# The last round of a triangular inverse in a two-layer kernel, computed on one 32x32 block a head instead of on masked 64x64 blocks

## The chip, the cores and the metric

The kernel runs on one core of a Trainium2 chip. The metric is device time in microseconds (us); three runs of the kernel before gave 3733.14, 3735.51 and 3737.32 us. The engines are called PE (tensor engine; its weight loads are PEld), DVE (vector engine), ACT (scalar engine), POOL (GpSimd) and SP (which issues the DMAs).

## The reference, cut to what matters

The program is two transformer-like blocks over 512 tokens of width 1024. The second block's even layer holds a recurrence with 12 heads of width 64, in two directions, over 768 tokens (256 of context and 512 of latents):

```
def rwkv7_scan(r, w, k, v, kk, bb, s0, reverse):
    def step(s, inp):
        r_t, w_t, k_t, v_t, kk_t, b_t = inp
        sa = jnp.einsum('bhij,bhj->bhi', s, kk_t)
        s = s * w_t[:, :, None, :] - sa[..., None] * b_t[:, :, None, :] + v_t[..., None] * k_t[:, :, None, :]
        return s, jnp.einsum('bhij,bhj->bhi', s, r_t)
```

The kernel does not step token by token. It cuts the tokens into 12 chunks of 64. Inside a chunk the term with `sa` couples each token to all tokens before it, which is a triangular system of 64 equations for each head; the kernel inverts its matrix (ones on the diagonal, a strictly triangular 64x64 part that holds products of `bb` and `kk`).

## The kernel before, in words

**Passes.** The function `rwkv` runs 12 passes, `products(i)`, one for each pair of heads `p` and direction `d` (`p, d = divmod(i, 2)`). The two heads of a pair lie in partitions 0 to 63 and 64 to 127, and `halves_matmul` issues one 64x64 product for each. Each pass is one `stage`: a block of all engines, closed by a barrier. The next pass begins on every engine only when the last engine has ended its part.

**Inside a pass.** First come the `units`, products whose results are masked and stored (`mats`, `ntrk`, `ax`, and `wb`). Then come 15 `rounds` of the inverse: 5 levels (block sizes 2, 4, 8, 16, 32) for each of 3 groups of 4 chunks. `buf.wb` holds for each chunk the inverse so far, transposed in columns 0 to 63 ("wt") and straight in columns 64 to 127. Round n of level b does this:

1. POOL: `off_diagonal(n)` multiplies the strict triangle in `mats` by a mask of the two off-diagonal bxb blocks of each 2bx2b block, into `off`.
2. PE: the Y product, `off` (weights) by the straight half of `wb`, into bank 0 or 1 of PSUM. The trace shows it as `second_wb,second_off`.
3. ACT: copies it to `y`.
4. PE, one turn of the loop later: the W product, `y` by `wt` (`second_wb,second_y`), and except in the last level also its straight twin (`second_y,second_wb`).
5. DVE: adds the result to `wb`. In the last level it adds only to the 64 columns of `wt`.

In the text Y(n), W(n) and mask(n) are these steps of round n; rounds 12, 13 and 14 are the last level. On PE the loop's order is Y(n), then what stands "beside", then W(n-1).

**Beside the rounds.** Two other pieces of work are dealt into fixed places of the same loop, on each engine: `Terms` (the elementwise terms of pass i+1, in long DVE instructions of 128x768) and `Recurrence` (the chunk-to-chunk state of pass i-1). A `step` of the recurrence is 12 small products on PE, then a `tensor_scalar` on DVE that makes the state `st` for the next step. Passes 1 to 10 have both; pass 0 has only `Terms`, pass 11 only `Recurrence`. The order in each engine's queue is fixed by this loop: no scheduler moves anything.

Of the kernel before, what the change touches and what calls it, by code (L numbers as in the profile page):

```python
# [11 lines left out]
ALU = mybir.AluOpType  # L12
# [26 lines left out]
N_SHIFT = 3 * RWKV_W + 256  # L39
CH = 64  # L40
NCH = T2 // CH
RET_HEADS = 8
DECAY = math.exp(-0.5)

# [14 lines left out]
def const_table():  # L59
# [46 lines left out]
    t["upper"] = np.concatenate([s < q, s <= q], 1)  # L106
    t["lower"] = np.concatenate([s > q, s >= q], 1)
    t["eye64"] = s == q
    for b in (1, 2, 4, 8, 16, 32):
        off = (s // (2 * b) == q // (2 * b)) * (s // b != q // b)  # L110
        t[f"up{b}"] = off * (s < q)
        t[f"lo{b}"] = off * (s > q)
# [1778 lines left out]
class Recurrence:  # L1891
# [33 lines left out]
    def slots(self, g):  # L1925
        first = slot_of(self.i, self.starts[g])
        return slice(first, first + 4)
# [134 lines left out]
def rwkv(nc, w, u_dram, o_dram, xc, common, psum, col, at, columns):  # L2062
# [4 lines left out]
    with ExitStack() as ctx:  # L2067
# [210 lines left out]
        def products(i):  # L2278
# [3 lines left out]
            ar, bk, starts = buf.ar[:, i % 3, :, :], buf.bk[:, i % 2, :, :], group_starts(d)  # L2282
            pair_mask = "upper" if d == 0 else "lower"
            pre_t, pre_f = ("up", "lo") if d == 0 else ("lo", "up")
            over = lambda name: mask(name).unsqueeze(1).to_broadcast([P, 4, mask(name).shape[1]])
            bank = lambda b, n: psum[:, b * 512:b * 512 + 4 * n].rearrange("p (c n) -> p c n", n=n)

# [11 lines left out]
            after_unit = lambda n: range(UNIT_PLACES * n // len(units), UNIT_PLACES * (n + 1) // len(units))  # L2299
            BANKS = 4  # L2300
            bank_y, bank_w = lambda n: bank(n % 2, CH), lambda n: bank(2 + n % 2, 2 * CH)
            names = "unit_ready taken_act taken_dve wt_scaled wt_begun wf_begun masked y_ready y_taken w_ready w_added "
            with stage(nc, names + Terms.NAMES + Recurrence.NAMES) as (block, sems):
                (unit_ready, taken_act, taken_dve, wt_scaled, wt_begun, wf_begun, masked, y_ready, y_taken, w_ready,
                 w_added) = sems[:11]
                terms = Terms(sems[11:11 + Terms.COUNT], i + 1, p - 1 if d == 1 and p else None)
                rec = Recurrence(nc, sems[11 + Terms.COUNT:], i - 1, buf, psum, eye)

                @block.sync
                def _(sp):  # L2310
# [3 lines left out]
                def _(pe):  # L2314
# [30 lines left out]
                    for n in range(len(rounds) + 1):  # L2345
                        if n < len(rounds):
                            level, g = rounds[n]
                            pe.wait_ge(masked, n + 1)
                            if level == 0:
                                pe.wait_ge(wf_begun, g + 1)  # L2350
                                pe.wait_ge(wt_begun, g + 1)
                            else:
                                pe.wait_ge(w_added, n - 2)
                            if n >= 2:
                                pe.wait_ge(y_taken, n - 1)
                            for c in range(4):
                                last = halves_matmul(nc, bank_y(n)[:, c, :], off[:, n % 2, c, :], buf.wb[:, slots(g).start + c, CH:])
                            last.then_inc(y_ready, 1)
                        beside(UNIT_PLACES + n)
                        if n:  # L2360
                            level, g = rounds[n - 1]
                            s0 = slots(g).start
                            pe.wait_ge(y_taken, n)
                            if n > 2:
                                pe.wait_ge(w_added, n - 2)
                            for c in range(4):
                                wt, y_ = buf.wb[:, s0 + c, 0:CH], y[:, own(g).start + c, :]
                                last = halves_matmul(nc, bank_w(n)[:, c, 0:CH], y_, wt)
                                if level < last_level:
                                    last = halves_matmul(nc, bank_w(n)[:, c, CH:], wt, y_)  # L2370
                            last.then_inc(w_ready, 1)

                @block.scalar
                def _(act):
# [18 lines left out]
                    for n in range(len(rounds) + 1):  # L2393
                        if n < len(rounds):
                            level, g = rounds[n]
                            act.wait_ge(y_ready, n + 1)
                            S.activation(y[:, own(g), :], bank_y(n), ACT.Identity).then_inc(y_taken, 1)  # L2397
                        beside(UNIT_PLACES + n)

                @block.vector  # L2400
                def _(dve):
# [19 lines left out]
                    for n in range(len(rounds) + 1):  # L2421
                        beside(UNIT_PLACES + n)
                        if n:
                            level, g = rounds[n - 1]
                            dve.wait_ge(w_ready, n)
                            n_cols = 2 * CH if level < last_level else CH
                            w_ = buf.wb[:, slots(g), 0:n_cols]
                            V.tensor_tensor(w_, w_, bank_w(n)[:, :, 0:n_cols], ALU.add).then_inc(w_added, 1)  # L2428

                @block.gpsimd  # L2430
                def _(pool):
# [18 lines left out]
                        for phase in terms.due(place, PLACES):  # L2450
                            terms.pool(pool, phase)
                    for n in range(len(rounds) + 1):
                        if 2 <= n < len(rounds):
                            off_diagonal(n)
                        for phase in terms.due(UNIT_PLACES + n, PLACES):
                            terms.pool(pool, phase)
# [512 lines left out]
```

## Time and profile before

| what | us |
|---|---|
| median of three runs | 3735.51 |
| the profiled execution, its time | 3739.27 |
| the profiled execution, its span from first to last instruction | 3737.5 |
| the stretch with the twelve passes (2360 to 3030 us of the span) | 670 |

A long name such as `L1881 PE MATMUL psum<-second_wb,second_off 64*64 64x64 f32` reads: line 1881, engine, operation, output, then the moving operand and the weights, the shape of the weights, and the shape of the moving operand. One product in f32 appears as two matmul records and two weight loads, so the 8 products of a group show as x16. Matmul records overlap their neighbours: a record's end is modelled, and the pace is read from the starts. `[0.78 <-DVE second_st L2022]` behind a row says that the engine had been idle for 0.78 us and that this DVE instruction released it.

### The profile page before, as it was taken

How to read it: one execution, taken by the hardware profiler on the slowest of the kernel's cores; microseconds unless marked ns; L12 is line 12 of the kernel's file. 1: busy time of each engine (PE TensorE's matmuls, PEld its weight loads, DVE VectorE, ACT ScalarE, POOL GpSimd, SP SyncE). 2: the span in 40 equal slices, each digit the busy share in tenths (PEclk: the TensorE clock that was granted, in tenths of full speed). 3: DMA queues.
4: the chain of work that ended last, by engine and by line, in shares of the span. 5: the costliest groups of instructions: out<-in, count | busy, mean ns of one | idle time of the engine just before them, and what ended most of it. 6: DMA issues, size and time to landing. Idle time of an engine off the chain costs nothing. (4 is left out here: it accounts for less than half of the span.)

```text
span 3737.5 us, 66286 instructions
## 1 busy us (share of the span) xinstructions
PE 3191.7 (85%) x28285; PEld 2513.8 (67%) x28285; DVE 1989.7 (53%) x2750; ACT 1124.0 (30%) x1783; POOL 1043.7 (28%) x608
## 2 busy tenths in 40 slices
PE   4998899999699988999855996799999978399886
PEld 2875567878476556887624884688888866279634
DVE  3678747860477874883204740566666632431252
ACT  2224424331323343332213221333333212322221
POOL 0322134544122222554200220444344311022100
PEclk7999899999899999999967998899999998799988
DMA  2331122333222122333171332000000021021101
GB/s 69 79 79 46 45 69 85 97 93 88 65 64 78 40 63 67 92 98 90 54 274 52 112 98 109 16 4 20 20 20 20 8 77 45 17 79 57 51 0 68
DMA packets 354104, 243.93 MB, mean 65 GB/s; under 512 B 22212, under 2 KB 330872, under 8 KB 353164
## 3 DMA queue, kind: packets, MB, share of 16 engines
q1 hardware_dynamic: 350398, 231.57, 20.7%
q10 hardware_dynamic: 3406, 8.04, 0.6%
q8 instruction: 227, 3.72, 0.4%
q14 instruction: 73, 0.60, 0.1%
HBM read 222.54 MB, written 17.04 MB: 64 GB/s over the span
## 5 line engine op out<-in xcount | busy, mean ns | idle before, releaser
L571 POOL TENSOR_TENSOR weights_lo<-weights_raw,weights_hi 128x1024 fp32r<-128x1024 f32 (+1 forms) x234 | 595.7, 2546 | 1151.4 <-ACT weights_hi L540 1151.4
L1167 PE MATMUL psum<-moving_hi,weights_hi 128*128 128x512 f32 x1488 | 609.0, 409 | 108.4 <-DVE weights_lo L571 61.3
L1167 PE MATMUL psum<-moving_lo,weights_hi 128*128 128x512 f32 x1488 | 589.0, 396 | 0.0
L1167 PE MATMUL psum<-moving_hi,weights_lo 128*128 128x512 f32 x1488 | 588.3, 395 | 0.0
L1167 PEld LDWEIGHTS psum<-moving_hi,weights_hi 128*128 128x128 f32 x1488 | 285.2, 192 | 226.2 <-issue 71.2
L540 ACT ACTIVATE weights_hi<-weights_raw 128x1024 fp32r<-128x1024 f32 (+2 forms) x250 | 253.7, 1019 | 280.5 <-PE psum L1167 240.4
L1167 PEld LDWEIGHTS psum<-moving_hi,weights_lo 128*128 128x128 f32 x1488 | 285.0, 192 | 61.8
L1167 PEld LDWEIGHTS psum<-moving_lo,weights_hi 128*128 128x128 f32 x1488 | 285.9, 192 | 59.2 <-issue 4.9
L2436 POOL TENSOR_TENSOR second_off<-second_mats,second_masks 128x256 f32<-128x256 f32 x180 | 141.1, 786 | 183.8 <-PE psum L1881 183.8
L1167 PE MATMUL psum<-hn_hi,even_hi 128*128 128x256 f32 (+1 forms) x480 | 162.9, 339 | 34.1 <-DVE even_lo L571 34.1
L571 POOL TENSOR_TENSOR even_lo<-even_raw,even_hi 128x1024 fp32r<-128x1024 f32 x28 | 67.4, 2408 | 362.8 <-ACT even_hi L540 362.8
L1881 PE MATMUL psum<-second_wb,second_y 64*64 64x64 f32 x2880 | 165.8, 218 | 0.4 <-issue 0.3
L1167 PE MATMUL psum<-hn_lo,even_hi 128*128 128x256 f32 (+1 forms) x480 | 162.7, 339 | 0.0
L1167 PE MATMUL psum<-hn_hi,even_lo 128*128 128x256 f32 (+1 forms) x480 | 162.4, 338 | 0.0
L2428 DVE TENSOR_TENSOR second_wb<-second_wb,psum 128x512 f32<-128x512 f32 (+1 forms) x180 | 113.2, 630 | 82.3 <-PE psum L1881 82.0
L719 DVE SCALAR_TENSOR_TENSOR cv<-u,columns,cv 128x512 f32<-128x512 f32 x88 | 154.8, 1759 | 3.1
L2397 ACT ACTIVATE second_y<-psum 128x256 f32<-128x256 f32 x180 | 68.7, 382 | 275.0 <-PE psum L1881 274.9
L1167 PE MATMUL psum<-hidden_hi,weights_hi 128*128 128x512 f32 x352 | 139.6, 397 | 7.5 <-POOL weights_lo L571 7.5
L1881 PE MATMUL psum<-second_y,second_wb 64*64 64x64 f32 x2304 | 141.9, 218 | 0.0
L1881 PEld LDWEIGHTS psum<-second_wb,second_y 64*64 64x64 f32 x2880 | 138.2, 135 | 1.7 <-issue 1.4
L1167 PE MATMUL psum<-hidden_lo,weights_hi 128*128 128x512 f32 x352 | 138.9, 395 | 0.0
L1167 PE MATMUL psum<-hidden_hi,weights_lo 128*128 128x512 f32 x352 | 138.9, 395 | 0.0
(430 smaller groups left out, 6890.1 us busy)
## 6 DMA issues: line engine op xcount, KB each, us to landing
weights_raw<-in_w_up SPq DMA_DIRECT2D x88, 512.0 KB, 3.9
weights_raw<-in_w_in SPq DMA_DIRECT2D x78, 512.0 KB, 3.8
ada_raw<-in_ada_w SPq DMA_DIRECT2D x12, 2048.0 KB, 18.6
odd_raw<-in_od_w_in SPq DMA_DIRECT2D x16, 1024.0 KB, 5.5
even_raw<-in_ev_w_in SPq DMA_DIRECT2D x30, 512.0 KB, 3.9
weights_raw<-in_w_down SPq DMA_DIRECT2D x32, 448.0 KB, 3.7
weights_raw<-in_w_o SPq DMA_DIRECT2D x16, 512.0 KB, 4.3
weights_raw<-in_w_down SPq DMA_DIRECT2D x16, 512.0 KB, 4.2
```

Of the source, the lines that this page charges most:

```text
L540: self.nc.scalar.activation(self.ring.hi[i % n][:, a:b], self.ring.raw[:, t % self.ring.landing, a:b], ACT.Identity)\
L571: ops.tensor_tensor(self.ring.lo[i % n][:, a:b], self.ring.raw[:, t % self.ring.landing, a:b], self.ring.hi[i % n][:, a:b].bitcast(F32), A ...
L719: nc.vector.scalar_tensor_tensor(y, x[:, 0:L], col("ffn_w", chunk), y, ALU.mult, ALU.add).then_inc(convolved, 1)
L1167: return nc.tensor.matmul(to, (hi, lo)[which][:, at:at + P], moving(k)[part], start=start and k == 0 and i == 0, stop=stop and k == n_k - ...
L1881: last = nc.tensor.matmul(out[ps, :], lhsT[ps, :], rhs[ps, :], start=start, stop=stop)
L2397: S.activation(y[:, own(g), :], bank_y(n), ACT.Identity).then_inc(y_taken, 1)
L2428: V.tensor_tensor(w_, w_, bank_w(n)[:, :, 0:n_cols], ALU.add).then_inc(w_added, 1)
L2436: G.tensor_tensor(off[:, n % 2, :, :], buf.mats[:, slots(g), 0:CH], over(f"{pre_t}{LEVELS[level]}"), ALU.mult)\
```

## The change

In the last level only one 32x32 block of the 64x64 matrix is off the diagonal and inside the triangle. The changed kernel computes only this block for each head. The Y product takes 32 rows and 32 columns of `mats` itself as weights, with no mask, and writes from one half of the head's partitions to the other half; the W product goes back the other way. ACT copies half as many columns. DVE copies the block into `wb`, where only zeros stand, in two instructions (one for each head, 32 partitions each) in place of one addition over 128 partitions. POOL's masks for rounds 12 to 14 and the two 64-column mask tables of block size 32 are gone. One more semaphore, `last_copied`, counts the copies.

```
+            first, other = (0, 1) if d == 0 else (1, 0)
+            half = lambda hf, j: slice(64 * hf + HB * j, 64 * hf + HB * j + HB)
+            columns_of = lambda j: slice(HB * j, HB * j + HB)
...
                         if n < len(rounds):
                             level, g = rounds[n]
-                            pe.wait_ge(masked, n + 1)
+                            if level < last_level:
+                                pe.wait_ge(masked, n + 1)
...
                             for c in range(4):
-                                last = halves_matmul(nc, bank_y(n)[:, c, :], off[:, n % 2, c, :], buf.wb[:, slots(g).start + c, CH:])
+                                x = slots(g).start + c
+                                if level < last_level:
+                                    last = halves_matmul(nc, bank_y(n)[:, c, :], off[:, n % 2, c, :], buf.wb[:, x, CH:])
+                                else:
+                                    for hf in range(2):
+                                        last = PE.matmul(bank_y(n)[half(hf, other), c, 0:HB], buf.mats[half(hf, first), x, columns_of(other)],
+                                                         buf.wb[half(hf, first), x, CH:][:, columns_of(first)], start=True, stop=True)
                             last.then_inc(y_ready, 1)
...
+                            adds = GROUPS * last_level
                             if n > 2:
-                                pe.wait_ge(w_added, n - 2)
+                                pe.wait_ge(w_added, min(n - 2, adds))
+                            if n - 2 > adds:
+                                pe.wait_ge(last_copied, 2 * (n - 2 - adds))
                             for c in range(4):
                                 wt, y_ = buf.wb[:, s0 + c, 0:CH], y[:, own(g).start + c, :]
-                                last = halves_matmul(nc, bank_w(n)[:, c, 0:CH], y_, wt)
                                 if level < last_level:
+                                    halves_matmul(nc, bank_w(n)[:, c, 0:CH], y_, wt)
                                     last = halves_matmul(nc, bank_w(n)[:, c, CH:], wt, y_)
+                                else:
+                                    for hf in range(2):
+                                        last = PE.matmul(bank_w(n)[half(hf, first), c, 0:HB], y_[half(hf, other), 0:HB],
+                                                         wt[half(hf, other), columns_of(other)], start=True, stop=True)
                             last.then_inc(w_ready, 1)
...
                             act.wait_ge(y_ready, n + 1)
-                            S.activation(y[:, own(g), :], bank_y(n), ACT.Identity).then_inc(y_taken, 1)
+                            n_cols = CH if level < last_level else HB
+                            S.activation(y[:, own(g), 0:n_cols], bank_y(n)[:, :, 0:n_cols], ACT.Identity).then_inc(y_taken, 1)
...
-                            n_cols = 2 * CH if level < last_level else CH
-                            w_ = buf.wb[:, slots(g), 0:n_cols]
-                            V.tensor_tensor(w_, w_, bank_w(n)[:, :, 0:n_cols], ALU.add).then_inc(w_added, 1)
+                            if level < last_level:
+                                w_ = buf.wb[:, slots(g), :]
+                                V.tensor_tensor(w_, w_, bank_w(n), ALU.add).then_inc(w_added, 1)
+                            else:
+                                for hf in range(2):
+                                    V.tensor_copy(buf.wb[half(hf, first), slots(g), columns_of(other)], bank_w(n)[half(hf, first), :, 0:HB])\
+                                        .then_inc(last_copied, 1)
...
                     for n in range(len(rounds) + 1):
-                        if 2 <= n < len(rounds):
+                        if 2 <= n < GROUPS * last_level:
                             off_diagonal(n)
```

On PE, near the end of pass 1: W(12), Y(14), step 10 of the recurrence, W(13). Before:

```order
L1881 MATMUL psum<-second_wb,second_y 64x64 x8
L1881 MATMUL psum<-second_wb,second_off 64x64 x8
L1881 MATMUL psum<-second_v_tok,second_mats 64x64 x2
L1881 MATMUL psum<-second_wau,second_mats 64x64 x2
L1881 MATMUL psum<-second_st,second_mr 64x64 x2
L1881 MATMUL psum<-second_ntrk,second_v_tok 64x64 x2
L1881 MATMUL psum<-second_mats,second_wau 64x64 x2
L1881 MATMUL psum<-second_mr,second_st 64x64 x2
L1881 MATMUL psum<-second_wb,second_y 64x64 x8
L1881 MATMUL psum<-second_v_tok,second_mats 64x64 x2
```

After (the line numbers move with the added lines):

```order
L2387 MATMUL psum<-second_wb,second_y 32x32 x8
L2367 MATMUL psum<-second_wb,second_mats 32x32 x8
L1882 MATMUL psum<-second_v_tok,second_mats 64x64 x2
L1882 MATMUL psum<-second_wau,second_mats 64x64 x2
L1882 MATMUL psum<-second_st,second_mr 64x64 x2
L1882 MATMUL psum<-second_ntrk,second_v_tok 64x64 x2
L1882 MATMUL psum<-second_mats,second_wau 64x64 x2
L1882 MATMUL psum<-second_mr,second_st 64x64 x2
L2387 MATMUL psum<-second_wb,second_y 32x32 x8
L1882 MATMUL psum<-second_v_tok,second_mats 64x64 x2
```

The places are the same; the three groups of 8 products of the last level are now 32x32, and they stand between groups of 64x64 products.

On DVE, in the same pass, the end of its queue: state 9, the result of W(12), a term of pass 2, state 10, W(13), a term, state 11, the output, W(14). Before:

```order
L2022 TENSOR_SCALAR second_st<-psum,second_decay 128x64
L2428 TENSOR_TENSOR second_wb<-second_wb,psum 128x4x64
L2237 TENSOR_TENSOR second_a<-second_kk,second_a 128x768
L2022 TENSOR_SCALAR second_st<-psum,second_decay 128x64
L2428 TENSOR_TENSOR second_wb<-second_wb,psum 128x4x64
L2239 TENSOR_TENSOR second_bk<-second_a,second_e 128x12x64
L2022 TENSOR_SCALAR second_st<-psum,second_decay 128x64
L2027 TENSOR_TENSOR second_o<-second_o,psum 128x256
L2428 TENSOR_TENSOR second_wb<-second_wb,psum 128x4x64
```

After:

```order
L2023 TENSOR_SCALAR second_st<-psum,second_decay 128x64
L2450 COPY second_wb<-psum 32x4x32 x2
L2238 TENSOR_TENSOR second_a<-second_kk,second_a 128x768
L2023 TENSOR_SCALAR second_st<-psum,second_decay 128x64
L2450 COPY second_wb<-psum 32x4x32 x2
L2240 TENSOR_TENSOR second_bk<-second_a,second_e 128x12x64
L2023 TENSOR_SCALAR second_st<-psum,second_decay 128x64
L2028 TENSOR_TENSOR second_o<-second_o,psum 128x256
L2450 COPY second_wb<-psum 32x4x32 x2
```

Each addition of 128x4x64 has become two copies of 32x4x32, in the same place of the queue.

## Rows read from the trace of the kernel before

**Rows 1.** Busy us (count) of PE, PEld, DVE, ACT, POOL; then PEclk, DMA share, GB/s
```profile
2360.00:3030.00 670.00, 621.94 (x16708) 577.23 (x16710) 417.94 (x666) 229.84 (x443) 275.98 (x310) 0.99 0.05 15
```

**Rows 2.** Groups of instructions in the same stretch; columns as on the page
```profile
L1881 PE MATMUL psum<-second_wb,second_off 64*64 64x64 f32 x2880 | 115.5, 218 | 3.4 <-POOL second_off L2436 2.1 <-issue 0.6 <-ACT second_ax L2390 0.6
...
L2436 POOL TENSOR_TENSOR second_off<-second_mats,second_masks 128x256 f32<-128x256 f32 x180 | 141.1, 786 | 183.8 <-PE psum L1881 183.8
...
L2428 DVE TENSOR_TENSOR second_wb<-second_wb,psum 128x256 f32<-128x256 f32 x36 | 15.0, 418 | 8.2 <-PE psum L1881 7.9
```

**Rows 3.** Timeline, tensor engine, end of a pass in direction 0; start us, us taken
```profile
2516.22 0.63 PE L1881 MATMUL psum<-second_wb,second_off 64*64 64x64 f32 x16
...
2521.27 0.63 PE L1881 MATMUL psum<-second_wb,second_y 64*64 64x64 f32 x15
...
2521.97 0.33 PE L1881 MATMUL psum<-second_v_tok,second_mats 64*64 64x64 f32 x4
...
2522.72 0.65 PE L1881 MATMUL psum<-second_wb,second_y 64*64 64x64 f32 x16
...
2524.40 1.15 PE L1881 MATMUL psum<-second_masks,second_bk 64*64 64x64 f32 x32 [1.04 <-PEq L187]
```

**Rows 4.** Timeline, vector engine and GpSimd, end of the same pass
```profile
2517.05 1.45 DVE L2235 SCALAR_TENSOR_TENSOR second_ar<-second_kk,second_e 128x768 f32<-128x768 f32 x1
...
2518.61 0.67 DVE L2428 TENSOR_TENSOR second_wb<-second_wb,psum 128x512 f32<-128x512 f32 x1
...
2520.30 0.42 DVE L2428 TENSOR_TENSOR second_wb<-second_wb,psum 128x256 f32<-128x256 f32 x1 [0.53 <-PE psum L1881]
...
2520.64 0.95 DVE L2237 TENSOR_TENSOR second_a<-second_kk,second_a 128x768 f32<-128x768 f32 x1
...
2521.94 0.42 DVE L2428 TENSOR_TENSOR second_wb<-second_wb,psum 128x256 f32<-128x256 f32 x1
...
2522.28 0.95 DVE L2239 TENSOR_TENSOR second_bk<-second_a,second_e 128x768 f32<-128x768 f32 x1
...
2523.67 0.41 DVE L2428 TENSOR_TENSOR second_wb<-second_wb,psum 128x256 f32<-128x256 f32 x1
...
2516.95 0.73 POOL L2436 TENSOR_TENSOR second_off<-second_mats,second_masks 128x256 f32<-128x256 f32 x1 [1.53 <-PE psum L1881]
```

**Rows 5.** Timeline, three engines, end of a pass in direction 1
```profile
2460.38 0.73 POOL L2436 TENSOR_TENSOR second_off<-second_mats,second_masks 128x256 f32<-128x256 f32 x1 [1.79 <-PE psum L1881]
...
2460.48 1.45 DVE L2233 TENSOR_TENSOR second_kk<-second_kk,second_tmp 128x768 f32<-128x768 f32 x1
...
2461.96 0.96 DVE L2235 SCALAR_TENSOR_TENSOR second_ar<-second_kk,second_e 128x768 f32<-128x768 f32 x1
...
2463.17 0.33 PE L1881 MATMUL psum<-second_v_tok,second_mats 64*64 64x64 f32 x4 [0.78 <-DVE second_st L2022]
...
2464.60 0.42 DVE L2428 TENSOR_TENSOR second_wb<-second_wb,psum 128x256 f32<-128x256 f32 x1 [0.53 <-PE psum L1881]
...
2467.96 0.41 DVE L2428 TENSOR_TENSOR second_wb<-second_wb,psum 128x256 f32<-128x256 f32 x1
```

**Rows 6.** Groups of instructions over the whole span, vector engine
```profile
L266 DVE COPY columns<-psum 128x128 f32<-128x128 f32 x3 | 0.8, 291 | 6.9 <-PE psum L280 6.9
```

**Rows 7.** Timeline, tensor engine, products of 128 and of 64 columns in a row
```profile
2417.96 1.92 PE L1881 MATMUL psum<-second_ar,second_bk 64*64 64x128 f32 x32
2419.71 0.63 PE L1881 MATMUL psum<-second_v_tok,second_ntrk 64*64 64x64 f32 x16
2420.18 0.63 PE L1881 MATMUL psum<-second_masks,second_ar 64*64 64x64 f32 x16
```

**Rows 8.** Timeline, tensor engine and its weight loads, around a product of another shape
```profile
2414.44 0.66 PE L1881 MATMUL psum<-second_bk,second_ar 64*64 64x64 f32 x16
...
2415.03 1.55 PE L2111 MATMUL psum<-second_lora,second_w 64*128 64x256 f32 x4
...
2416.51 0.19 PEld L1881 LDWEIGHTS psum<-second_v_tok,second_ntrk 64*64 64x64 f32 x4 [0.76 <-issue]
```

More of the change, by code:

```diff
@@ L41 @@
 NCH = T2 // CH
+HB = CH // 2
 RET_HEADS = 8
@@ L108, in const_table @@
     t["eye64"] = s == q
-    for b in (1, 2, 4, 8, 16, 32):
+    for b in (1, 2, 4, 8, 16):
         off = (s // (2 * b) == q // (2 * b)) * (s // b != q // b)
@@ L2301, in products @@
             bank_y, bank_w = lambda n: bank(n % 2, CH), lambda n: bank(2 + n % 2, 2 * CH)
-            names = "unit_ready taken_act taken_dve wt_scaled wt_begun wf_begun masked y_ready y_taken w_ready w_added "
+            names = "unit_ready taken_act taken_dve wt_scaled wt_begun wf_begun masked y_ready y_taken w_ready w_added last_copied "
             with stage(nc, names + Terms.NAMES + Recurrence.NAMES) as (block, sems):
                 (unit_ready, taken_act, taken_dve, wt_scaled, wt_begun, wf_begun, masked, y_ready, y_taken, w_ready,
-                 w_added) = sems[:11]
-                terms = Terms(sems[11:11 + Terms.COUNT], i + 1, p - 1 if d == 1 and p else None)
-                rec = Recurrence(nc, sems[11 + Terms.COUNT:], i - 1, buf, psum, eye)
+                 w_added, last_copied) = sems[:12]
+                terms = Terms(sems[12:12 + Terms.COUNT], i + 1, p - 1 if d == 1 and p else None)
+                rec = Recurrence(nc, sems[12 + Terms.COUNT:], i - 1, buf, psum, eye)
                 @block.sync
```

## The prediction

> **What bounds the kernel now.** The change touches only the twelve passes of the recurrence. I first read the busy time by stretch: in these 670 us PE is busy for 621.94 us, DVE for 417.94 us and POOL for 275.98 us, and the granted clock is 0.99 of full speed, the 2.4 GHz level [rows 1]. So PE is nearly full, but the slack of 48 us is where a pass begins and ends, and a gain counts only if it reaches the barrier at the end of a pass.
>
> Then the groups of instructions. The last level is a small part of the rounds: of the 180 masks and Y products it has 3 in each pass, 36 in all, and the 36 additions of 128x256 on DVE are its own, 15.0 us busy [rows 2]. PE waited for a mask for only 2.1 us in all [rows 2], so taking masks away frees PE of nothing that can be seen.
>
> Then the timeline of the last microseconds of a pass, since only what ends last there counts. In a pass of direction 0 PE goes from group to group without a gap up to W(13) at 2521.27, waits shortly before the last step of the recurrence at 2521.97, and issues W(14) at 2522.72. It is done with it 0.65 us later, at 2523.37. DVE, however, works without a gap from the result of W(12) at 2520.30 (before which it waited 0.53 us for PE) through the terms of 0.95 us each at 2520.64 and 2522.28, up to the addition of W(14) at 2523.67, which ends at 2524.08 [rows 3, 4]. The next pass starts on PE at 2524.40 [rows 3]. So **DVE ends the pass**, and the chain is: PE up to W(12), then DVE.
>
> In a pass of direction 1 the chain starts earlier. PE waits 0.78 us for a state of the recurrence, which stands on DVE behind the terms of 1.45 and 0.96 us [rows 5]. From there it goes through step 9 and W(12) on PE (addition at 2464.60) to the last addition, 2467.96 to 2468.37 [rows 5]. Other passes of the same direction show the same pattern.
>
> **The change, part by part.**
>
> *Masks.* Mask(12) and mask(13) run while DVE works on PSUM or on one source, and nothing waits for them: nothing. Mask(14) is different. It runs 2460.38 to 2461.11, and the DVE term that begins at 2460.48 takes 1.45 us. The term behind it, of the same size, takes 0.96 us [rows 5]. In direction 0 it is the other term, L2235, that coincides with mask(14) (2516.95, 0.73 us) and takes 1.45 us at 2517.05 [rows 4], while the same line takes 0.96 us in direction 1, where no mask runs [rows 5]. I conclude that the mask delays this term by 1.45 - 0.96 = 0.49 us, and that it goes with the mask. In direction 1 this lies on the chain: -0.49. In direction 0 it does not: the addition behind it, at 2518.61 [rows 4], needs W(11), which PE delivers only shortly before, so the gain ends there.
>
> *The products.* 8 products of 64 columns take 2420.18 - 2419.71 = 0.47 us. 16 products of 128 columns take 1.75 us, 0.875 us for 8 [rows 7]. On the straight line through both, 8 products of 32 columns would take 0.47 - (0.875 - 0.47)/2 = 0.27 us, a saving of 0.20. The other end is no saving at all. The nearest row is that of 64 columns, and two such groups cost more than one of 128 columns (0.94 against 0.875), which hints at a fixed part in each product. I take 0.40 us, a saving g = 0.07 for each group.
>
> The Trainium skill (TensorEngine Tiling (Array Packing), Instruction Overhead) says that every matmul carries some 60 cycles, so that one of a single column takes as long as one of 60. No row here has a 64-row product of fewer than 64 columns. By that rule g is 0, and the sum below would come to +5.5 us; by the straight line it would be below zero.
>
> *The change of shape.* The small products stand between 64x64 products. The trace has no change between 32 and 64, but one between 64x64 and 64x128: the 8 products from 2414.44 should be followed at 2414.91 and are followed at 2415.03, 0.12 us late. Then come 768 columns, 1.31 us at the pace of rows 7 (1.75/8 for a pair of 128), so the next could start at 2416.34. Its weights are loaded at 2416.51, after the loader had been idle for 0.76 us [rows 7, 8]. So a change costs 0.12 to 0.17 us there, part of it the load of 128 columns that nothing covers, which is smaller with 32. The ends are 0 and 0.17; I take t = 0.10. A pass has 5 changes into the small shape (before Y(12), Y(13), W(12), W(13), W(14); W(12) and Y(14) stand together) and 4 out of it that something in the pass follows.
>
> The same page (Key Properties) says that changing the tiling mode drains TensorE. Row 8's two gaps agree with it in kind; whether 64 to 32 rows is priced alike, no row here shows. This rule speaks against the change. At 0.17 for each change it would make the sum some 3 us larger.
>
> *ACT* copies half the columns of Y. The copy runs beside a step of the recurrence, and its result is needed only behind it: nothing.
>
> *DVE.* An addition of 128x256 takes 0.42 us and the next instruction starts 0.34 us after it (2520.30 to 2520.64) [rows 4]. Nearest to a copy of 32x4x32 is the copy of 128x128 out of PSUM, 0.291 us [rows 6]. With the same overlap of 0.08 it holds DVE for 0.21, two of them for 0.42 to 0.44. So each group costs DVE 0.10 more, and the very last one ends 0.09 later. The lower end is two copies of about 0.15 (-0.04), the upper one two as long as the addition (+0.34). The trace has no 32-partition copy; I take +0.10. They lie on the chain in every pass with terms.
>
> *The sum.* Direction 1 (5 passes): -0.49 for the term; W(12) +t - g = +0.03, so its result comes 0.46 earlier; copies +0.10, so the next term starts 0.36 earlier. Then W(13) decides: PE has done W(12) and Y(14) (-0.14), changed shape out and in (+0.20) and done W(13) itself (-0.07) since; it was 0.05 ahead of DVE before and comes 0.39 earlier now. Copies +0.10, last one +0.09: the pass ends 0.20 us earlier. Direction 0 (5 passes): Y(12) and Y(13) each +2t - g = +0.13, W(12) +0.03, so 0.29 later; copies make it 0.39; W(13) comes 0.32 later by the same count and holds the chain; copies +0.10 and +0.09: 0.51 later. The first pass has no recurrence, DVE is its bound, and the term's gain and the dearer parts nearly cancel: +0.1. The last pass has no terms, PE is its bound: 9t - 6g + 0.09 = +0.57. In all 5 x (-0.20) + 5 x 0.51 + 0.1 + 0.57 = **+2.2 us**. The table of masks is a little smaller and is loaded beside two longer loads: nothing. The clear of one more semaphore is POOL's, which is idle then.
>
> The profiled execution took 3739.27 us, 1.8 us more than its span of 3737.5 and 3.8 us more than the median. Its sum is 3741.5; from the median, 3735.5 + 2.2 = 3737.7 us.
>
> **Rivals.**
> 1. *Small products are truly small and a change of shape is free* (g = 0.20, t = 0). For it: PE overlaps the two heads' products already. Then direction 1 ends 0.5 earlier, direction 0 some 0.5 earlier, the last pass 1.1, the first 0.3: -6.4 us, 3729. Against it: the gaps in rows 8. Chance 0.13.
> 2. *A floor, no saving* (g = 0, t = 0.10): direction 0 +0.85, direction 1 0, the last pass +1.0, the first +0.2: +5.5 us, 3741. Chance 0.17.
> 3. *Slower by the change of shape*: PE empties at each change, t = 0.17, with g = 0. Direction 0 +1.34, direction 1 +0.22, the ends 2.0 together: +9.8 us, 3745.3. It decides from about t = 0.13 on with g = 0. For it: both gaps of rows 8. Against: part of those is the wide weight load. Chance 0.12.
> 4. *Copies as dear as additions*: 0.24 more in each of 3 groups of 11 passes, +7.9 on top of +2.2: 3745.6, slower. Against it: 0.291 for 128 columns. Chance 0.03.
> 5. *The term keeps its 1.45 us*, so that its price is not the mask's: direction 1 loses the 0.49 again, +2.4: 3740. Chance 0.07.
>
> My forecast, g between 0.02 and 0.14 with t near 0.10, has 0.48.
>
> **How the numbers follow.** What a measurement of this kernel can tell from no change is about 0.2%, 7.5 us. My forecast, rivals 2 and 5 and most of rival 1 lie within it. Faster needs rival 1 with still cheaper copies: 0.07. Slower: most of rival 3, rival 4 and the tail of rival 2: 0.13. Same: 0.80. The range leaves out half of rival 1 and most of rivals 3 and 4 and allows for the spread of the runs (4 us): 3730 to 3744.
>
> **What the profile would show.** Right: the term beside the former mask(14) at 0.96 us in passes 1 to 10; groups of 8 small products every 0.40 us; a gap of about 0.1 us at each change of shape; copies of about 0.25 to 0.3 us; ends of passes 0.2 us earlier in direction 1 and 0.5 us later in direction 0. Wrong: groups of 0.27 us without gaps, or gaps of 0.2 us and more, copies of 0.4 us, a term that stays at 1.45 us, or a wait of PE for `last_copied`.

## The result, and the profile after

| | median, us | lowest to highest | runs | ratio to before, 95% interval |
|---|---|---|---|---|
| before | 3735.38 | 3733.14 to 3737.32 | 4 | |
| after | 3757.89 | 3756.89 to 3760.64 | 4 | 1.0063 [1.0047, 1.0079] |

The changed kernel is slower by 0.63%, 22.5 us, where +2.2 us was forecast. Its profiled execution took 3756.89 us, with a span of 3755.1 us. The same view of the twelve passes as [rows 1], and the groups that belong to the last level:

```profile
2360.00:3030.00 670.00, 609.93 (x16099) 562.32 (x16101) 415.65 (x681) 222.26 (x432) 248.47 (x272) 0.97 0.05 15
```

```profile
L2459 POOL TENSOR_TENSOR second_off<-second_mats,second_masks 128x256 f32<-128x256 f32 x142 | 113.6, 802 | 132.9 <-PE psum L1882 132.9
...
L2450 DVE COPY second_wb<-psum 32x128 f32<-32x128 f32 x66 | 18.9, 286 | 5.9 <-PE psum L2387 4.5
L2367 PE MATMUL psum<-second_wb,second_mats 32*32 32x32 f32 x528 | 14.9, 194 | 0.0
L2387 PE MATMUL psum<-second_wb,second_y 32*32 32x32 f32 x528 | 14.5, 193 | 0.2 <-ACT second_y L2416 0.2
```

The stretch of [rows 1] is fixed in time, and after the change it ends 17 us before the last pass does. So the two are compared once more from the first product of pass 0 to the first one behind pass 11, first before, then after (columns as in [rows 1]):

```profile
2366.58:3026.45 659.87, 618.39 (x16624) 573.79 (x16625) 411.80 (x660) 228.20 (x439) 275.98 (x310) 1.00 0.05 15
2370.11:3046.56 676.45, 625.42 (x16624) 577.20 (x16625) 415.36 (x696) 224.64 (x439) 249.93 (x274) 0.97 0.05 15
```

The passes are 16.6 us longer. PE issues as many products and is busy for 7 us more with them, though 72 groups of 8 (Y and W of three rounds in twelve passes) are smaller; the granted clock is 0.97 instead of 1.00. The copies take 286 ns each, in pairs, where one addition took 418 [rows 2]. PE's waits for a barrier grow from 22.5 to 30.8 us in all, those for a state of the recurrence from 15.3 to 18.9.

The tensor engine at the end of pass 1 (direction 1), timeline:

```profile
2466.22 0.28 PE L1882 MATMUL psum<-second_y,second_wb 64*64 64x64 f32 x4
2466.43 0.44 PE L2367 MATMUL psum<-second_wb,second_mats 32*32 32x32 f32 x16
2466.80 0.33 PE L1882 MATMUL psum<-second_v_tok,second_mats 64*64 64x64 f32 x4
...
2470.19 0.34 PE L2387 MATMUL psum<-second_wb,second_y 32*32 32x32 f32 x10
...
2470.44 0.35 PE L2367 MATMUL psum<-second_wb,second_mats 32*32 32x32 f32 x11
2470.72 0.33 PE L1882 MATMUL psum<-second_v_tok,second_mats 64*64 64x64 f32 x4
...
2473.50 0.44 PE L2387 MATMUL psum<-second_wb,second_y 32*32 32x32 f32 x16
2475.82 1.12 PE L1882 MATMUL psum<-second_masks,second_rkv 64*64 64x64 f32 x16 [1.88 <-PEq L188]
```

A small group of 16 records, 0.19 us each, starts at 2466.43 and has its last record end 0.44 us later, so its 15 steps take 0.25 us and the group 0.27. The four records ahead of it, at 0.12 us for four of 64x64, should be followed at 2466.34 and are followed 0.09 later. The product behind it could start at 2466.70 and starts 0.10 later. W(12) and Y(14), side by side, run into each other: with the change out of the shape they take 0.53 us, 0.43 without. The last row is the first product of pass 2: PE waited 1.88 us for it.

The vector engine in the same microseconds, to the end of the pass:

```profile
2467.15 0.95 DVE L2234 TENSOR_TENSOR second_kk<-second_kk,second_tmp 128x768 f32<-128x768 f32 x1
2468.14 0.96 DVE L2236 SCALAR_TENSOR_TENSOR second_ar<-second_kk,second_e 128x768 f32<-128x768 f32 x1
...
2470.68 0.61 DVE L2450 COPY second_wb<-psum 32x128 f32<-32x128 f32 x2 [0.43 <-PE psum L2387]
2471.32 0.96 DVE L2238 TENSOR_TENSOR second_a<-second_kk,second_a 128x768 f32<-128x768 f32 x1
2472.31 0.28 DVE L2023 TENSOR_SCALAR second_st<-psum,second_decay 128x64 f32<-128x64 f32 x1
2472.63 0.61 DVE L2450 COPY second_wb<-psum 32x128 f32<-32x128 f32 x2
2473.27 0.96 DVE L2240 TENSOR_TENSOR second_bk<-second_a,second_e 128x768 f32<-128x768 f32 x1
2474.24 0.28 DVE L2023 TENSOR_SCALAR second_st<-psum,second_decay 128x64 f32<-128x64 f32 x1
2474.44 0.41 DVE L2028 TENSOR_TENSOR second_o<-second_o,psum 128x256 f32<-128x256 f32 x1
2474.88 0.61 DVE L2450 COPY second_wb<-psum 32x128 f32<-32x128 f32 x2
```

The first term takes 0.95 us where [rows 5] has 1.45. Two copies hold the engine for 0.64 us (2470.68 to 2471.32), where the addition held it for 0.34. From W(12)'s result to the end of the pass DVE needs 4.81 us, against 3.77 in [rows 5] (2464.60 to 2468.37).

So far this is a matter of half a microsecond a pass. The rest shows only in the windows over the first 6 us of each pass (columns as in [rows 1]). Passes 1 to 6 after, then passes 1 to 3 before:

```profile
2415.21:2421.21 6.00, 6.00 (x84) 6.00 (x85) 1.26 (x2) 0.60 (x1) 0.00 (x0) 0.52 0.62 199
2475.82:2481.82 6.00, 6.00 (x113) 5.91 (x114) 1.59 (x3) 1.64 (x4) 0.37 (x1) 0.73 0.02 4
2533.46:2539.46 6.00, 6.00 (x99) 5.88 (x100) 1.81 (x3) 1.56 (x3) 0.68 (x1) 0.72 0.81 252
2592.95:2598.95 6.00, 6.00 (x88) 6.00 (x90) 0.69 (x1) 0.98 (x2) 0.00 (x0) 0.54 0.02 4
2651.73:2657.73 6.00, 6.00 (x126) 5.12 (x128) 1.81 (x3) 2.92 (x4) 2.22 (x4) 1.00 0.83 251
2709.60:2715.60 6.00, 6.00 (x112) 5.97 (x112) 1.38 (x2) 1.30 (x3) 0.01 (x1) 0.72 0.02 4
```

```profile
2411.27:2417.27 6.00, 6.00 (x125) 5.12 (x127) 1.81 (x3) 2.91 (x4) 2.21 (x4) 1.00 0.63 199
2468.69:2474.69 6.00, 6.00 (x125) 5.12 (x127) 1.81 (x3) 2.83 (x5) 1.75 (x3) 1.00 0.02 5
2524.40:2530.40 6.00, 6.00 (x126) 5.12 (x127) 1.81 (x3) 2.91 (x4) 2.22 (x4) 1.00 0.82 256
```

PE is busy for all 6 us in each of them, and does as few as 84 records instead of 125: a busy share says nothing of the pace. The clock column does: a mean of 0.72 says that PE ran at the lower level, 1.2 GHz, for part of these 6 us and at 2.4 GHz for the rest. Behind the longer idle time most passes have such a stretch at or shortly behind their start. Before, every one of passes 1 to 11 has 1.00; only pass 0, behind 10.38 us of idle time, has less (0.77).

### The profile page after: what moved, and what is told of

It is laid out like the page before. It is cut to its first block and busy times, and to the rows that moved or that the text cites. A ratio compares the mean times of both kernels' runs of the same rounds, so it can differ in the third digit from the quotient of the medians.

```text
span 3755.1 us, 66298 instructions
## 1 busy us (share of the span) xinstructions
PE 3200.0 (85%) x28285; PEld 2517.8 (67%) x28285; DVE 1994.4 (53%) x2786; ACT 1120.5 (30%) x1783; POOL 1018.3 (27%) x572
## 5 line engine op out<-in xcount | busy, mean ns | idle before, releaser
L2459 POOL TENSOR_TENSOR second_off<-second_mats,second_masks 128x256 f32<-128x256 f32 x144 | 115.0, 801 | 135.9 <-PE psum L1882 135.9
L2416 ACT ACTIVATE second_y<-psum 128x256 f32<-128x256 f32 (+1 forms) x180 | 65.0, 361 | 268.4 <-PE psum L1882 210.5
L1882 PE MATMUL psum<-second_wb,second_y 64*64 64x64 f32 x2304 | 141.8, 218 | 0.0
L2447 DVE TENSOR_TENSOR second_wb<-second_wb,psum 128x512 f32<-128x512 f32 x144 | 98.4, 684 | 75.9 <-PE psum L1882 75.9
L1483 DVE SCALAR_TENSOR_TENSOR conv<-conv_padded,columns,conv 128x512 f32<-128x512 f32 x120 | 134.9, 1124 | 3.5
```

The lines of the kernel that those rows point to most:

```text
L1483: chain.then(nc.vector.scalar_tensor_tensor(conv[:, i, :], padded[:, i, k:k + L], col("conv_w", 2 * k + i), conv[:, i, :], ALU.mult, ALU.add))
L1882: last = nc.tensor.matmul(out[ps, :], lhsT[ps, :], rhs[ps, :], start=start, stop=stop)
L2416: S.activation(y[:, own(g), 0:n_cols], bank_y(n)[:, :, 0:n_cols], ACT.Identity).then_inc(y_taken, 1)
L2447: V.tensor_tensor(w_, w_, bank_w(n), ALU.add).then_inc(w_added, 1)
L2459: G.tensor_tensor(off[:, n % 2, :, :], buf.mats[:, slots(g), 0:CH], over(f"{pre_t}{LEVELS[level]}"), ALU.mult)\
```

## The experiments

Each kernel was profiled once and timed beside the kernel before. The ratio is to the runs of before that stood beside it (their medians: 3735.21, 3735.10 and 3735.77 us); "median" is in us as measured. A pass is counted here from its first product on PE to that of the next. "Idle" is PE's idle time ahead of a pass, behind one of direction 1 / of direction 0. "Low" counts those of passes 2 to 11 whose first 6 us have a granted clock below 1.00, in the text a low start. "Length" is the median of those of passes 1 to 10 that start at 1.00, direction 1 / direction 0. "Sum" is from the start of pass 0 to that of pass 11. All in us.

| kernel | idle | low of 10 | length | sum | median | ratio |
|---|---|---|---|---|---|---|
| before | 1.05 / 1.05 | 0 | 57.42 / 55.71 | 611.3 | 3735.38 | |
| after | 1.88 / 1.61 | 6 | 57.87 / 56.19 | 627.3 | 3757.89 | 1.0063 |
| r1_after | 1.88 / 1.61 | 7 | 57.94 / 56.19 | 630.0 | 3756.23 | 1.0058 [1.0045, 1.0072] |
| f1_fill | 0.57 / 0.31 | 0 | 57.89 / 56.23 | 618.0 | 3745.54 | 1.0033 [1.0020, 1.0045] |
| f2_half_fill | 1.16 / 0.88 | 0 | 57.88 / 56.18 | 618.0 | 3744.67 | 1.0026 [1.0015, 1.0037] |
| c1_copies | 1.75 / 1.48 | 3 | 58.42 / 56.25 | 624.8 | 3746.30 | 1.0036 [1.0022, 1.0050] |
| i1_idle | 1.90 / 1.90 | 6 | 58.28 / 56.32 | 627.0 | 3752.47 | 1.0046 [1.0032, 1.0059] |
| s1_small | 1.03 / 1.03 | 0 | 57.12 / 55.45 | 609.0 | 3732.91 | 1.0003 [0.9994, 1.0012] |
| m1_nomask | 1.05 / 1.05 | 0 | 56.93 / 55.60 | 608.6 | 3732.03 | 0.9993 [0.9984, 1.0002] |
| n1_no_copies | 1.03 / 1.03 | 2 | 57.09 / 55.38 | 612.1 | 3732.89 | 0.9992 [0.9983, 1.0001] |
| a1_act | 0.92 / 0.91 | 0 | 56.19 / 55.07 | 601.6 | 3726.77 | 0.9976 [0.9966, 0.9985] |
| i2_act_idle | 1.27 / 1.27 | 2 | 56.55 / 55.47 | 609.4 | 3732.05 | 0.9990 [0.9981, 0.9999] |
| a2_act_fill | 0.31 / 0.31 | 0 | 56.90 / 55.79 | 608.8 | 3736.23 | 1.0004 [0.9995, 1.0013] |
| b1_fill | 0.31 / 0.31 | 0 | 57.85 / 55.85 | 613.8 | 3744.62 | 1.0023 [1.0012, 1.0034] |

In before, c1_copies and m1_nomask pass 5 is about 1 us longer than its like (58.46 before): PE stops once for 0.71 to 0.73 us, 7 us into the pass and at full clock, and the profile shows no release. For c1_copies, where only passes 1 and 5 of direction 1 start at 1.00, the table has pass 1; for i1_idle only pass 1 does. (Where an expectation speaks of 8 of the 11 passes after, the windows show 7: six in the table, and pass 1.)

**Is it the clock?** Theory: the longer idle time ahead of a pass lets the clock fall. Rival: the direct costs of the copies and of the shape. A filler behind W(14) keeps PE busy while DVE ends the pass; nothing reads its products, and it delays nothing that DVE does:

```
+                    for k in range(10):        # f2_half_fill: range(5)
+                        halves_matmul(nc, bank(k % 2, CH)[:, k // 2 % 4, :], eye, eye)
```

> The changed kernel with ten pairs of 64x64 products of a constant (1.2 us of PE work, nobody reads the result) behind W(14) of every pass, while PE would wait for the barrier. Left out: nothing. Theory A (most of the loss is the tensor clock, which falls to half at the start of a pass because PE does little before it): the first 6 us of each pass stay at a granted clock of 1.0 and only the 0.5 us for each pass remain, which the passes with an unbroken clock show: 3741 us, 0.996 of the changed kernel's time. Theory B (the loss is in the copies, the semaphores or the barrier itself): no change, 3758 us.

> The changed kernel with five pairs of unread products behind W(14) instead of ten: 0.6 us. PE's idle time before a pass falls from 1.9 and 1.6 us to about 1.2 and 0.9, near that of the kernel before (1.05). Theory A (idle time that goes on longer than before is what lets the clock fall): 3745 us, as with ten pairs. Rival (it takes as much PE work as ten pairs make): clock falls in several passes, 3750 us or more.

Both take back some 12 us of the 22.5; f1_fill, expected at 3741 us, came out 4.5 us above that. The end of pass 1 and the next two starts in f2_half_fill, timeline and windows:

```profile
2468.01 0.44 PE L2387 MATMUL psum<-second_wb,second_y 32*32 32x32 f32 x16
2468.39 0.80 PE L1882 MATMUL psum<-second_masks 64*64 64x64 f32 x20
2470.34 0.68 PE L1882 MATMUL psum<-second_masks,second_rkv 64*64 64x64 f32 x16 [1.16 <-PEq L188]
```

```profile
2470.34:2476.34 6.00, 6.00 (x126) 5.12 (x128) 1.81 (x3) 2.83 (x5) 1.75 (x3) 1.00 0.03 7
2526.53:2532.53 6.00, 6.00 (x126) 5.12 (x128) 1.81 (x3) 2.92 (x4) 2.22 (x4) 1.00 0.81 253
```

The lengths at full clock are those of after to 0.04 us, so the filler changed nothing but the starts. (In f1_fill the clock fell once within pass 10, which took 58.15 us; f2_half_fill has no such pass, but its pass 1 started at 0.50 behind 2.02 us of idle time.) More work made the kernel faster. What stays, 57.88 - 57.42 and 56.18 - 55.71 a pass, is the direct cost. (By the medians the fillers leave 9 to 10 us. In the sums, which have 6.7 for both, the ten direct costs are 4.7; most of the rest is the low start of pass 1 in f2_half_fill and the fall within pass 10 in f1_fill.)

The opposite: the kernel before, with its idle time lengthened and nothing of the change in it, by one unread addition at the end of DVE's queue:

```
+                    V.tensor_tensor(unread[:, :], reset[:, :], reset[:, :], ALU.add)
```

> The kernel before, all its PE work, masks and additions in place, with one unread vector addition of 128x768 (0.95 us) at the end of each pass: PE's idle time before the next pass grows from 1.05 to about 1.95 us, as in the changed kernel, and nothing else changes. Theory A (the longer idle time alone lets the clock fall): 0.9 us for each of 12 passes, 11 us, and on top of it 1.5 to 3 us for each pass that starts at half clock: 3750 to 3765 us. Rival (it takes less PE work as well): clock 1.0 at every start, 3746 us.

The end of pass 2, and the first 6 us of passes 3 and 2, timeline and windows:

```profile
2525.23 0.63 PE L1881 MATMUL psum<-second_wb,second_y 64*64 64x64 f32 x16
2527.77 1.97 PE L1881 MATMUL psum<-second_masks,second_bk 64*64 64x64 f32 x32 [1.90 <-PEq L187]
...
2526.51 0.95 DVE L2431 TENSOR_TENSOR second_unread<-second_reset 128x768 f32<-128x768 f32 x1
```

```profile
2527.77:2533.77 6.00, 6.00 (x99) 5.87 (x100) 1.81 (x3) 1.58 (x3) 0.69 (x1) 0.72 0.82 252
2471.49:2477.49 6.00, 6.00 (x126) 5.12 (x127) 1.81 (x3) 2.83 (x5) 1.75 (x3) 1.00 0.02 4
```

The addition costs 0.86 and 0.61 us a pass by the lengths at full clock, and five of passes 1 to 10 are longer by another 1.6 to 1.8 since they start low (59.88 against 58.28): 8.3 us of the 15.7 in the sum. So the clock falls without any of the change's instructions.

**Which part makes the idle time?** The copies alone, in the kernel before (the products still 64 wide):

```
-                            w_ = buf.wb[:, slots(g), 0:n_cols]
-                            V.tensor_tensor(w_, w_, bank_w(n)[:, :, 0:n_cols], ALU.add).then_inc(w_added, 1)
...
+                                for hf in range(2):
+                                    made = V.tensor_copy(buf.wb[half(hf, first), slots(g), columns_of(other)],
+                                                         bank_w(n)[half(hf, first), :, columns_of(other)])
```

> The kernel before with one part of the change: the two copies of 32x4x32 in place of each last-level addition; masks and 64x64 products stay. The result is the same. Theory A (copies cost DVE 0.30 us more for each group, not 0.10, all on the chain; and a later end of DVE leaves PE idle for longer): 0.7 us for each of 11 passes, +8 us, 3743 us; and if the longer idle time before the next pass is enough for the clock to fall, up to +20. Rival (copies are hidden, the small products alone matter): 3735 us, no change.

```profile
L2435 DVE COPY second_wb<-psum 32x128 f32<-32x128 f32 x72 | 20.6, 286 | 7.8 <-PE psum L1882 6.9
```

The first 6 us of pass 3:

```profile
2521.82:2527.82 6.00, 6.00 (x99) 5.87 (x100) 1.81 (x3) 1.63 (x3) 0.73 (x1) 0.72 0.82 251
```

They cost 1.00 and 0.54 us a pass, and with them come the longer idle time and three low starts. Then the other parts alone: only the small products (the stale columns are added too), only the masks left out (full products on the unmasked `mats`), and both together, which is the change without the copies (and with the full copy of Y):

> The kernel before with one part of the change: the 32x32 products in the last level; masks, the full copy of Y and the 128x256 addition stay (the addition then also adds stale columns, so the inverse is not the reference's). Theory A (the small products make PE do less before the barrier, and that alone lets the clock fall): clock below 1.0 at the start of several passes, +5 to +12 us. Rival (it takes the longer idle time too, which the copies make): clock stays at 1.0, and the pass ends at most 0.3 us earlier or later: 3733 to 3738 us.

> The kernel before with one part of the change: no masks in the last level, the 64x64 products take the unmasked matrix (so the inverse is not the reference's). Expected by all theories: the vector term beside mask(14) takes 0.96 instead of 1.45 us; passes of direction 1 end 0.49 us earlier, those of direction 0 as before: -2.5 us, 3733 us. Rival (the term's length isn't the mask's): no change in the term.

> The changed kernel with one part undone: the 128x256 addition on DVE in place of the two copies (it also adds stale columns, so the inverse is not the reference's), the full copy of Y, and no last_copied. The small products, and no masks, stay. Theory A (the copies are what costs, directly and through the clock): passes of direction 1 at 56.6 us, of direction 0 at 55.3, PE idle for about 1.05 us before a pass, clock 1.0 in nearly all: 3728 us, faster than before. Rival (small products and missing masks together take enough work from PE for the clock to fall, as in the changed kernel): several passes start at half clock, 3740 us or more.

None of the three is told from before by its interval, so what follows rests on the lengths of passes in one execution each. By length, no mask gives 0.49 us in direction 1, exactly the term's gain, and 0.11 in direction 0; the small products give 0.30 and 0.26. In m1_nomask the term stands at 0.95 us, and W(12) comes so much earlier, and not more:

```profile
2460.72 0.95 DVE L2233 TENSOR_TENSOR second_kk<-second_kk,second_tmp 128x768 f32<-128x768 f32 x1
...
2464.34 0.42 DVE L2431 TENSOR_TENSOR second_wb<-second_wb,psum 128x256 f32<-128x256 f32 x1 [0.53 <-PE psum L1881]
```

n1_no_copies missed its expectation of 3728 us, and two of its starts are low behind 0.93 and 1.03 us of idle time. Its length in direction 1 is only 0.33 below before, where the two parts alone add up to 0.79. It rests on three passes: two of them lost 0.4 us within their first 15 us, for which no cause was found, and the third took 56.71, 0.71 less than before.

So by the lengths of the passes the masks and the products were gains, and the copies turned them into a loss.

**The copies elsewhere.** a1_act is the changed kernel with the copies on ACT, which is idle there:

```
+                        if n > GROUPS * last_level:
+                            level, g = rounds[n - 1]
+                            act.wait_ge(w_ready, n)
+                            for hf in range(2):
+                                S.activation(buf.wb[half(hf, first), slots(g), columns_of(other)], bank_w(n)[half(hf, first), :, 0:HB],
+                                             ACT.Identity).then_inc(last_copied, 1)
```

> The changed kernel with the copies on ACT, which is idle there, in place of DVE. All outputs as the reference. Theory A: DVE loses its last-level work from the chain (0.64 us for each group), PE ends each pass; direction 1 ends about 1.2 us earlier than before the change and direction 0 about 1.0; the idle time of PE before a pass is about 0.9 us and the clock stays: 3724 us. Rival (less PE work close to the barrier is enough for the clock to fall at any idle time): at least half of the passes start at half clock, 3735 us or more.

The end of its pass 1, timeline of three engines:

```profile
2464.89 0.56 ACT L2422 ACTIVATE second_wb<-psum 32x128 f32<-32x128 f32 x2 [1.34 <-PE psum L2387]
...
2466.30 0.56 ACT L2422 ACTIVATE second_wb<-psum 32x128 f32<-32x128 f32 x2 [0.55 <-PE psum L2387]
2467.52 0.56 ACT L2422 ACTIVATE second_wb<-psum 32x128 f32<-32x128 f32 x2 [0.66 <-PE psum L2387]
...
2467.15 0.42 DVE L2028 TENSOR_TENSOR second_o<-second_o,psum 128x256 f32<-128x256 f32 x1
...
2467.03 0.44 PE L2387 MATMUL psum<-second_wb,second_y 32*32 32x32 f32 x16
2468.39 0.68 PE L1882 MATMUL psum<-second_masks,second_rkv 64*64 64x64 f32 x16 [0.92 <-PEq L188]
```

ACT ends the pass now, at 2468.08; DVE is done at 2467.57. Passes 2 to 11 all start at full clock. **This kernel beats both**: 3726.77 us, 0.24% faster than before (interval 0.15 to 0.34%).

**Controls.** The longer idle time in a1_act, and the filler where it was not needed:

> a1_act with the same unread vector addition at the end of each pass. DVE ends some 0.5 us before ACT there, so PE's idle time grows from 0.92 to about 1.35 us and each pass is 0.4 us longer: 3732 us if the clock holds. Theory A (the clock falls between 1.05 and 1.5 us of idle time): it falls in a few passes, 3732 to 3740 us. Rival (with the small products any longer idle time suffices): in most passes, 3745 us or more.

> As a1_act, with the ten pairs of unread 64x64 products behind W(14) of every pass (1.2 us). Theory A: the clock holds everywhere; the filler ends some 0.3 us later than the pass would, so 3727 us if the clock held without it, and less than a1_act only if it didn't. Rival: the filler delays every barrier by its full length, 3738 us.

> A control: the kernel before with the same ten pairs of unread products behind W(14) of every pass. Theory A (the filler only acts through the clock, which is whole at the start of the passes anyway): PE's end moves from 0.7 us before DVE's end to 0.5 us after it, so each pass ends 0.3 to 0.5 us later: 3740 us. Rival (the filler brings a gain of its own, which would make f1_fill no evidence): below 3733 us.

With 1.27 us of idle time instead of 0.92, two starts in ten are low (at 0.72), and the sum grows by 7.9 us. The filler costs where it ends the pass itself: 0.43 and 0.14 us a pass in b1_fill, 0.71 and 0.72 in a2_act_fill, where 0.3 was expected, and 3736.23 us is nearer the rival's 3738 than 3727. But a pass does not pay for the whole filler of 1.2 us, as the rival had it. This gives 2.5 and 7.3 us in the sums. The median of b1_fill, however, is 9.5 us above that of before beside it, and what the other 7 us are I can't say (the interval begins at +4.5). So the filler is a probe and no remedy.

**The changed kernel again**, beside the runs of the last batch:

> The changed kernel again, so that the fillers, the idle time and it are measured on one chip: 3758 us by every theory; the number of passes that start below full clock may differ from the first profile, where it was 8 of 11 (passes 1 to 11).

The same result within the spread (3751.45 to 3763.01 us), and the same six low starts, with that of pass 10 besides.

## Why the prediction was wrong

**The step that failed** is the sum: it made the end of the pass on DVE the only thing that a longer pass costs ("DVE ends the pass", then a start 0.2 us earlier or 0.5 later). It said nothing of PE, which waits for that end. [rows 1] gave the clock as 0.99 and [rows 3] the idle time ahead of the pass as 1.04 us; neither was asked what would become of the one if the other grew. (The slack of 48 us was put where passes begin and end; of PE's waits in the twelve passes 22.5 us are for a barrier, 10.4 of these ahead of pass 0, and 15.3 for states of the recurrence.) The rows of before could have told of the risk, by pass 0 at 0.77 behind 10.38 us of idle time, but not that 0.6 to 0.8 us more would be enough. After, 1.88 and 1.61 us of idle time are followed by low starts in six of ten passes. Such a start costs 1.5 to 1.9 us where the 6 us show 0.72 or 0.73, and 2.6 to 2.7 us at 0.52 or 0.54. The six low starts among passes 1 to 10 (that of pass 11 falls outside the sum) cost 11.9 us, measured against 57.87 and 56.18.

The account of the sum: 11.9 for the clock, 5 x 0.45 + 5 x 0.48 = 4.65 for the ten passes, 0.4 for pass 0, less 1.04 by which one pass of before happened to be longer than its like: 15.9 us, which is 627.3 - 611.3. Executions differ by about 3 us in it (r1_after has 18.7). The two profiled executions differ by 17.6 us in their spans. The rest of the 22.5 between the medians comes from which execution was profiled: before, it was one 3.9 us above its median, after, one 1.0 below. That the clock is a cause is shown, by f2_half_fill and i1_idle from both sides. What exactly makes it fall in one pass and not in the next is not.

**Masks**: right. The term takes 0.95 us, and m1_nomask gives 0.49 us in direction 1. In direction 0, where nothing was forecast, it gives 0.11.

**The products**: right in kind, too small. g is 0.20 (0.47 - 0.27), the end of the range that rival 1 has, not 0.07; and W(12) with Y(14) took 0.43 for both where 0.80 was counted. The rule of the Trainium skill (TensorEngine Tiling (Array Packing), Instruction Overhead) that the prediction weighed, by which g would be 0, does not hold for these groups: on alternating 32x32 blocks, 32 columns cost 0.27 us for 8 products where 64 cost 0.47.

**The change of shape**: right, 0.09 into it and 0.10 out of it, for t = 0.10.

**The copies**: the mis-sized term. Each group costs 0.28 to 0.30 more, not 0.10, and the last one ends 0.18 to 0.20 later, not 0.09. The overlap of 0.08 was taken over from the additions of 128 partitions and is not there: the second copy follows 0.32 us behind the first. Rival 4, given 0.03, is thus right on the size of one term, with +0.20 more where it had 0.24.

**Ends of passes**: f1_fill shows them at full clock. Vector engine, its copies of W(12) and W(14), pass 2 (which starts at 2465.94) and pass 3 (at 2522.13):

```profile
2517.26 0.60 DVE L2452 COPY second_wb<-psum 32x128 f32<-32x128 f32 x2 [0.44 <-PE psum L2387]
...
2521.21 0.59 DVE L2452 COPY second_wb<-psum 32x128 f32<-32x128 f32 x2
...
2574.86 0.61 DVE L2452 COPY second_wb<-psum 32x128 f32<-32x128 f32 x2 [0.43 <-PE psum L2387]
...
2579.07 0.61 DVE L2452 COPY second_wb<-psum 32x128 f32<-32x128 f32 x2
```

Direction 0: W(12) comes 51.32 us into the pass, 0.29 earlier than before (2520.30 - 2468.69 = 51.61), where 0.29 later was counted; from there to the end it takes 4.54 instead of 3.78 us. The pass is 0.48 longer. That agrees with the forecast 0.51 by two errors that cancel. Direction 1: W(12) 0.60 earlier (52.73 for 53.33; forecast 0.46), but 4.82 instead of 3.77 us behind it: 0.45 longer instead of 0.20 shorter. Of these 1.05 us the copies are 0.81; the other 0.24 stands in two places where DVE's next instruction follows 0.1 us later than before (2473.27 to 2474.24, 2474.44 to 2474.88), and its cause stays open.

So even with every price right the sum would have been +5 us, near 3740 and still "no change": the larger part of the loss came from the clock.

No rival came near 3757.89 us; the dearest two stand at 3745. Rivals 1 and 2 ask about g and t alone, and s1_small answers for g = 0.20 with t = 0.10. Rival 3 fails on t. Rival 5 fails on the term. Two slips in the working change nothing: by the count given for direction 1, W(13) in direction 0 comes 0.35 later and not 0.32, which makes the sum +2.4; and t = 0.17 in every change would add some 4 us, not 3.

## What to carry to other kernels

A delay at a barrier is to be priced twice: as time, and as idle time of the tensor engine behind which it may start at half clock; a row with the granted clock of the first microseconds after each wait shows whether a kernel pays it already. How near it is to paying no such row shows: before had 1.00 throughout, and 0.85 us more of idle time sufficed (i1_idle). One unread instruction at the end of a stage can tell. Cutting a copy out of PSUM down to fewer partitions saved next to nothing here (286 ns for 32x128, 291 for 128x128 [rows 6]), and cutting it in two cost the second one whole. If the engine that ends a stage is the one that gets the longer work, give that piece to an idle engine: here ACT turned +0.63% into -0.24%. And two kernels whose passes differ in length are compared from event to event, not over the same microseconds of their spans.

## What the hardware showed that was not expected

- The granted clock fell behind idle times of PE of less than 2 us in a stretch where PE is busy for 92% of the time (625.42 of 676.45 us). In the profiled executions, starts of passes 2 to 11: none of 30 was low at 0.30 to 0.57 us of idle time (f1_fill, a2_act_fill, b1_fill), 2 of 60 at 0.88 to 1.33 (before, f2_half_fill, a1_act, m1_nomask, s1_small, n1_no_copies), 2 of 10 at 1.27, 3 of 10 at 1.48 to 1.88 (c1_copies), and 19 of 30 at 1.6 to 2.2 (after, r1_after, i1_idle). The length of the idle time alone does not settle it: all three low starts of c1_copies stand behind 1.48 us, none behind 1.75. And pass 1 of a1_act started at 0.72 behind 0.91 us. Nor has every low start its fall ahead of it: pass 6 after had full clock for its first 1.5 us. The Trainium skill (TensorE: Matmul & The Clock Gate, Why this matters for your kernels) warns of idle gaps between bursts of matmuls, since the clock then returns to half; the trace agrees in kind (0.52 to 0.73 above, behind 1.6 to 3.0 us).
- Groups of eight 32x32 products in f32 take 0.27 us, 34 ns a product, 59 for a 64x64 one; two neighbouring groups overlap (0.43 for both).
- Copies of 32 partitions by 128 columns out of PSUM: 286 ns on DVE, 0.32 us apart; on ACT 0.56 us for two, 268 ns each in the mean.
